# Two transformer blocks in one kernel: the first modulation in column quarters, three projection chunks computed together

## The chip, the cores and the metric

The kernel runs on one core of a Trainium2 chip. Its engines are TensorE (PE in the rows; its loading of weights is PEld), VectorE (DVE), ScalarE (ACT), GpSimd (POOL, unused here) and SyncE (SP), which here does nothing but issue the DMAs. The metric is the device time of one execution, in microseconds (us); less is better.

## The reference

Two blocks run one behind the other on x, 256 rows by 2048. The stretch that changes is the head of the first, with the memory projection of the second, which depends on nothing and is done there too:

```python
# first block
ada = silu(c) @ w_ada + b_ada                    # [2048] @ [2048, 6*2048]
shift_m, scale_m, gate_m, shift_f, scale_f, gate_f = split(ada, 6)
h = rms_norm(x, g_pre_mix) * (1 + scale_m) + shift_m
z = h @ w_in                                     # [256, 2048] @ [2048, 3920]
... mixers (a latent attention and a gated linear attention) on z, w_out, residual, gated FFN
# second block, its memory side
kv = rms_norm(mem_2, ln_mem_2) @ w_xkv_2         # [256, 2048] @ [2048, 1024]
... mixers, cross attention on kv, gated FFN
```

Everything is float32. Each column of `h` needs its own column of shift_m and scale_m, and these need all 2048 rows of `w_ada` (16 k-tiles of 128 rows).

## The kernel before

**Slabs.** All weights come as *slabs* of 1 MB: 128 partitions by 2048 values, four slots (`raw`), one DMA each (`slab`, L398). A slot is issued again once DVE has finished with the slab four places earlier (semaphore `slab_done`). Projection slabs hold four k-tiles of 490 or 512 columns (DMA pieces of about 2 KB); a `w_ada` slab holds one k-tile of 2048 columns (pieces of 8 KB). "A slab" below means one of `w_ada`, "z slab" one of `w_in`, "xkv slab" one of `w_xkv_2`.

**Precision in two halves.** A product in full precision is made of three in a reduced form. ACT rounds a projection slab to `wh` (`hi`, L555), DVE takes the rest, `wl = raw - wh` (`lo`, L1633), and PE adds `wh*XTh`, `wl*XTh` and `wh*XTl` into a bank (`slab_mm`, L1045 to L1047; 24 matmuls a slab, four k-tiles by two row blocks by three). `XTh` and `XTl` are the activations, transposed and split the same way. `wh` and `wl` have two slots each, so ACT rounds a slab only when PE has used the one two before it.

**Modulation.** PE does not multiply `silu(c) @ w_ada`: DVE adds each A slab, scaled by one value of c per partition, to an accumulator of 2048 columns (`ada`, L1650 to L1654), and PE then sums `ACC` over the partitions with 16 one-column products (`mod_sum`, L1082), which DVE turns into shift, gain or gate (`mod_fin`).

**Order around the change.** All of it is written out by hand, for each engine by itself, and every queue runs in order:

1. The rows of mem are normed (ACT, DVE), turned by PE through two banks and split (`turn`, `turn_hi`, `turn_lo`). DVE does eight A slabs before and between.
2. The xkv slabs (two chunks of four), with A slabs of shift_m between those of the first chunk and of scale_m between those of the second. x is normed and turned in this stretch.
3. Seven more A slabs, `mod_sum(1)`, then the gain and shift on the turned x and its split (L1796), all 16 k-tiles.
4. The projection z: eight chunks of 490 columns, four slabs each, a loop of two times four chunks. Two A slabs of gate_m per chunk.
5. Behind it SP issues the slab of `w_uq`, three small loads and `rel_scratch<-relrow`, a 3 MB write of a table to DRAM, and then the 16 A slabs of shift_f. DVE computes rope angles, consumes the first two of these (`ada_some(2)`) and only then copies `aT` out of a bank, on which the gated linear attention's first product (L1146) waits.

## Time and profile before

| | |
|---|---|
| median of 3 runs | 2922.84 us (2920.22 to 2924.76) |
| the profiled execution, its own time | 2926.01 us |
| its span in the profile | 2924.2 us |
| PE busy | 2685.9 us (92%) |
| DVE busy | 1663.4 us (57%) |
| ACT busy | 1157.8 us (40%) |
| mean granted clock of TensorE | 0.954 of full |
| read from HBM | 559.59 MB |

The profile is of one execution. "Idle before" an instruction is the time its engine had nothing to do before it, with what ended that time. The part that changes lies in the first 334 us of the span; what stands behind it is the same code in both kernels, but for semaphore counts.

### The profile page before, as it was taken

The page shows a single profiled execution, that of the slowest core. Times are in us where ns is not written, and L with a number is a line of the kernel's source. Part 1 is how long each engine was busy: PE and PEld are TensorE (multiplying, and loading weights), DVE is VectorE, ACT ScalarE, POOL GpSimd, SP SyncE. Part 2 cuts the span into 40 slices and gives each one's busy share as a digit, 9 for nine tenths or more (in the row PEclk, how much of TensorE's full clock was granted, in tenths as well). Part 3 has the DMA queues.
Part 4 walks back from the last instruction along what each step waited for, and adds up shares of the span by engine and source line. Part 5 has one row for each costly group of instructions (what it writes and reads, how often), then busy time and mean ns, then how long its engine had stood idle before and what let it go on. Part 6 is the DMA issues. An engine that isn't in the chain of part 4 may idle for free.

```text
span 2924.2 us, 31137 instructions
## 1 busy us (share of the span) xinstructions
PE 2685.9 (92%) x12176; PEld 2194.6 (75%) x12176; DVE 1663.4 (57%) x1601; ACT 1157.8 (40%) x1200; POOL 0.2 (0%) x4
## 2 busy tenths in 40 slices
PE   3789769969999999999899999899889999999997
PEld 2578637757888888887788777787667888888886
DVE  6766565855666455555543666555564555555555
ACT  2333244433333333333433444434553333333333
POOL 0000000000000000000000000000000000000000
PEclk9789869979999999999899999999999999999999
DMA  8968843945777555555373444454435555555553
GB/s 329 352 236 286 226 187 110 336 156 189 250 253 260 172 191 192 190 185 171 127 224 118 147 142 132 139 201 160 157 101 185 189 186 187 186 191 192 190 186 129
DMA packets 253356, 565.93 MB, mean 194 GB/s; under 512 B 9647, under 2 KB 52557, under 8 KB 240094
## 3 DMA queue, kind: packets, MB, share of 16 engines
q1 hardware_dynamic: 253278, 564.87, 57.7%
q8 instruction: 52, 0.85, 0.1%
q14 instruction: 26, 0.21, 0.0%
HBM read 559.59 MB, written 5.24 MB: 193 GB/s over the span
## 4 chain that ended last, share of the span: by engine, by line
PE 78%; DVE 8%; ACT 5%; DMA 4%; issue 4%; SPq 1%; DVEq 0%; ACTq 0%
PE bank L1045 23%; PE bank L1047 23%; PE bank L1046 23%; ACT wh L555 3%; DVE wl L1633 2%; DVE ACC L1654 2%; DMA raw<-in_w_ada 2%; DVE ROWB L1633 1%; DMA raw<-in_w_out 1%; DMA raw<-in_w_xkv 1%; PE bank L1016 1%; PE bank L1451 1%; DVE X L1754 1%; PE bank L1503 1%; PE bank L1082 1%
## 5 line engine op out<-in xcount | busy, mean ns | idle before, releaser
L1633 DVE TENSOR_TENSOR wl<-raw,wh 128x2048 fp32r<-128x2048 f32 (+2 forms) x430 | 975.3, 2269 | 912.2 <-ACT wh L555 911.5
L555 ACT ACTIVATE wh<-raw 128x2048 fp32r<-128x2048 f32 (+2 forms) x430 | 816.0, 1898 | 1260.6 <-PE bank L1047 1158.8
L1045 PE MATMUL bank<-wh,XTh 128*128 128x512 f32 (+2 forms) x2712 | 1077.6, 397 | 46.3 <-DVE wl L1633 36.7
L1046 PE MATMUL bank<-wl,XTh 128*128 128x512 f32 (+2 forms) x2712 | 1064.1, 392 | 0.0
L1047 PE MATMUL bank<-wh,XTl 128*128 128x512 f32 (+2 forms) x2712 | 1063.5, 392 | 0.0
L1045 PEld LDWEIGHTS bank<-wh,XTh 128*128 128x128 f32 x2712 | 520.4, 192 | 158.4 <-DVE wl L1633 31.5
L1047 PEld LDWEIGHTS bank<-wh,XTl 128*128 128x128 f32 x2712 | 518.9, 191 | 103.4
L1046 PEld LDWEIGHTS bank<-wl,XTh 128*128 128x128 f32 x2712 | 520.9, 192 | 99.0
L1045 PE MATMUL bank<-wh,HTh 128*128 128x512 f32 x704 | 276.7, 393 | 9.4 <-DVE HTl L1633 3.6
L1047 PE MATMUL bank<-wh,HTl 128*128 128x512 f32 x704 | 274.2, 389 | 0.0
L1046 PE MATMUL bank<-wl,HTh 128*128 128x512 f32 x704 | 274.1, 389 | 0.0
L1045 PEld LDWEIGHTS bank<-wh,HTh 128*128 128x128 f32 x704 | 132.1, 188 | 46.5 <-issue 14.4
L1047 PEld LDWEIGHTS bank<-wh,HTl 128*128 128x128 f32 x704 | 132.2, 188 | 27.7
L1046 PEld LDWEIGHTS bank<-wl,HTh 128*128 128x128 f32 x704 | 132.2, 188 | 26.6
L1654 DVE SCALAR_TENSOR_TENSOR ACC<-raw,cT,ACC 128x2048 f32<-128x2048 f32 x60 | 141.0, 2350 | 7.2 <-DMA raw<-in_w_ada 2.2
L1633 DVE TENSOR_TENSOR ROWB<-ROWB,bank 128x512 f32<-128x512 f32 x176 | 112.6, 681 | 10.9 <-PE bank L1047 9.0
L1650 DVE SCALAR_TENSOR_TENSOR ACC<-raw,cT,ACC 128x2048 f32<-128x2048 f32 x32 | 75.2, 2351 | 4.2 <-DVE wl L1633 1.6
L1016 PE MATMUL bank<-CON,ROWB 128*128 128x128 f32 x96 | 19.1, 355 | 48.2 <-ACT ROWB L548 17.1
L821 ACT ACTIVATE HTh<-bank 128x512 fp32r<-128x512 f32 x44 | 23.9, 595 | 90.4 <-PE bank L1331 90.4
L1016 PEld LDWEIGHTS bank<-CON,ROWB 128*128 128x128 f32 x96 | 14.2, 180 | 53.3 <-ACT ROWB L548 18.0
L548 ACT ACTIVATE XTh<-bank,vT 128x256 fp32r<-128x256 f32 x70 | 28.8, 471 | 47.7 <-PE bank L1016 47.6
L1016 PE MATMUL bank<-CON,X 128*128 128x128 f32 x96 | 19.8, 375 | 27.3 <-DVE X L1754 17.2
(289 smaller groups left out, 1313.4 us busy)
## 6 DMA issues: line engine op xcount, KB each, us to landing
raw<-in_w_ada SPq DMA_DIRECT2D x96, 1024.0 KB, 6.7
raw<-in_w_ffn_gate SPq DMA_DIRECT2D x44, 1024.0 KB, 5.1
raw<-in_w_ffn_up SPq DMA_DIRECT2D x44, 1024.0 KB, 5.2
raw<-in_w_ffn_down SPq DMA_DIRECT2D x44, 1024.0 KB, 5.1
raw<-in_w_gate SPq DMA_DIRECT2D x44, 1024.0 KB, 5.1
raw<-in_w_up SPq DMA_DIRECT2D x44, 1024.0 KB, 5.1
raw<-in_w_down SPq DMA_DIRECT2D x44, 1024.0 KB, 5.1
raw<-in_w_in SPq DMA_DIRECT2D x32, 1024.0 KB, 5.1
```

The costliest lines, as they stand in the source:

```text
L555: act.activation(wh[:, st.lin % 2, 0:width], raw[:, st.raw % 4, 0:width], ACT.Copy).then_inc(hi_made, 1)
L1016: mm = pe.transpose(PB[4 + g % 2][:, SEQ * k + P * r:SEQ * k + P * r + P], src(r, 2 * b + k), ident)
L1045: pe.matmul(out_, hi_t[:, k, rows], w[0][:, q, :], start=first and q == 0, stop=False)
L1046: pe.matmul(out_, hi_t[:, k, rows], w[1][:, q, :], start=False, stop=False)
L1047: mm = pe.matmul(out_, lo_t[:, k, rows], w[0][:, q, :], start=False, stop=last and q == n - 1)
L1082: mm = pe.matmul(PB[7][:, k:k + 1], ACC[:, P * k:P * k + P], ones[:, 0:1], start=True, stop=True)
L1451: pe.matmul(PB[2 + u % 2][:, 0:2 * nk].rearrange("p (b n) -> p b n", b=2), QT(i, par, r), KT2(g, nk), start=True, stop=True).then_inc(S("n ...
L1503: pe.matmul(PB[7][:, HD * b:HD * b + HD], pT[:, u % 2, P * blk_:P * blk_ + P], Z2[:, k, c0:c0 + HD], start=k == 0, stop=k == r)
L1633: return dve.tensor_tensor(out_, a, b, op)
L1650: ins = dve.scalar_tensor_tensor(ACC[:, :], w, cT[:, bass.ds(k0 + k, 1)], ACC[:, :], ALU.mult, ALU.add)
L1654: ins = dve.scalar_tensor_tensor(ACC[:, :], w, cT[:, k:k + 1], ACC[:, :], ALU.mult, ALU.add)
L1754: dve.scalar_tensor_tensor(x, y, nstat[:, j, 2, r:r + 1], x, ALU.mult, ALU.add).then_inc(S("x_added"), 1)
```

## The change

- **A slabs of shift_m and scale_m by column quarters.** A slab is now four k-tiles by 512 columns, in pieces of 2 KB (`ada_part`). DVE handles it in four instructions of 512 columns; even and odd k-tiles go to two partial sums, so that none reads what the one in front of it wrote. Quarter q of the columns is complete after four slabs of each.
- **Sums by quarter.** `mod_parts(q)` sums both, adding the partial sums in the bank: 16 one-column products per quarter. Shift and gain of four k-tiles follow (`mod_part`), then gain and shift on four k-tiles of x by DVE (`h_gained`) and, now computed by ACT for itself from the same numbers, the rounded half (`h_hi`), and `h_lo`.
- **Three chunks together.** Chunks 0 to 2 of z stay open in banks 0 to 5: as soon as a quarter of h is there, its four k-tiles are multiplied with one slab of each of the three chunks. One quarter is: xkv slab, z0, two A, z1, two A, z2, A, xkv slab, three A. The K/V projection of the memory moves to banks 6 and 7. The last five chunks go one after the other, with one A slab of gate_m behind each of the first 16 of their 20 slabs; these loops are written out instead of run as loops.
- **Memory rows turned first.** mem is turned as it is loaded, at once and over four banks, and the norm factor of its rows is applied to the product (`scale=mem_scale(r)`). x is normed behind it and turned over four banks too.

The core of the diff:

```diff
+ZK = 3
+XKV = [(i // 4, i % 4) for i in range(8)]
+WIDE = {"mem", "x"}
+def turn_bank(name, b):
+    return 4 + (b % 4 if name in WIDE else (TURN0[name] + b) % 2)
...
+        def mod_at(q):
+            return PB[5 if q < 3 else 4][:, (496, 496, 504, 496)[q]:(504, 504, 512, 504)[q]]
+        def z_banks(c):
+            return (2 * c, 2 * c + 1) if c <= ZK else (2 * (c % 2), 2 * (c % 2) + 1)
... SP
-            for k in range(8):
-                ada(0, k)
-            for c in range(2):
-                for s in range(4):
-                    cols("w_xkv_2", s, 512 * c, 512)
-                    for k in range(8 + 2 * s, 10 + 2 * s) if c == 0 else range(3 * s, 3 * s + 3):
-                        ada(c, k)
+            def ada_part(v, q, s):
+                slab(W["w_ada"][:, 4 * s:4 * s + 4, v * D + 512 * q:v * D + 512 * q + 512], (4, 512), False)
+            for v in range(2):
+                for s in range(4):
+                    ada_part(v, 0, s)
+                if v == 0:
+                    xkv(0)
+            for q in range(4):
+                xkv(2 * q + 1)
+                for c in range(ZK):
+                    cols("w_in", q, ZC * c, ZC)
+                    if q < 3 and c < 2:
+                        for s in range(2 * c, 2 * c + 2):
+                            ada_part(0, q + 1, s)
+                if q < 3:
+                    ada_part(1, q + 1, 0)
+                    xkv(2 * q + 2)
+                    for s in range(1, 4):
+                        ada_part(1, q + 1, s)
+            for n in range(4 * (ZN - ZK)):
+                cols("w_in", n % 4, ZC * (ZK + n // 4), ZC)
+                if n < KT:
+                    ada(2, n)
... ACT
-            norm_stats("mem", lambda r: MEM[:, r, :], D)
-            norm_rows("mem", lambda r: MEM[:, r, :], lambda r: ROWB[:, r, :])
+            turn_hi("mem", MTh, gain=vT[:, V_LN_MEM:V_LN_MEM + KT])
             act.wait_ge(S("x_in"), 16)
             norm_stats("x", lambda r: X[:, r, :], D)
+            norm_rows("x", lambda r: X[:, r, :], lambda r: XN[:, r, :])
...
+            def h_hi(q):
+                act.wait_ge(S("mod_ready"), 2 * q + 2)
+                for b in (2 * q, 2 * q + 1):
+                    for kt in (2 * b, 2 * b + 1):
+                        ins = act.activation(XTh[:, kt, :], XS[:, kt, :], ACT.Identity, scale=modA[:, 1, kt:kt + 1],
+                                             bias=modA[:, 0, kt:kt + 1])
... PE
+            def mod_parts(q):
+                pe.wait_ge(slab_done, st.raws())
+                for v in range(2):
+                    for k in range(4):
+                        o = mod_at(q)[:, 4 * v + k:4 * v + k + 1]
+                        for par in range(2):
+                            c0 = 512 * (2 * v + par) + P * k
+                            mm = pe.matmul(o, ACC[:, c0:c0 + P], ones[:, 0:1], start=q == 0 and par == 0, stop=par == 1,
+                                           skip_group_check=True)
+                    mm.then_inc(S("mod_sum"), 1)
+            for q in range(4):
+                mod_parts(q)
+                xkv(2 * q + 1)
+                pe.wait_ge(S("x_lo"), 2 * q + 2)
+                for c in range(ZK):
+                    slab_mm(z_banks(c), ALL[4 * q:4 * q + 4], ZC, q == 0, q == 3)
...
+                if q < 3:
+                    st.next(False)
+                    xkv(2 * q + 2)
... DVE
+            def ada_part(v, q, s):
+                dve.wait_ge(landed[st.raw % 4], st.landed())
+                for t in range(4):
+                    part = ACC[:, 512 * (2 * v + t % 2):512 * (2 * v + t % 2) + 512]
+                    w, c = raw[:, st.raw % 4, 512 * t:512 * t + 512], cT[:, 4 * s + t:4 * s + t + 1]
+                    if s == 0 and t < 2:
+                        ins = dve.tensor_scalar(part, w, c, None, ALU.mult)
+                    else:
...
+                        ins = dve.scalar_tensor_tensor(part, w, c, part, ALU.mult, ALU.add)
+            for q in range(4):
+                lo()
+                mod_part(q)
+                h_gained(q)
+                h_lo(q)
+                for c in range(ZK):
+                    lo(4 * ZC)
+                    if q < 3 and c < 2:
+                        for s in range(2 * c, 2 * c + 2):
+                            ada_part(0, q + 1, s)
+                if q < 3:
+                    ada_part(1, q + 1, 0)
+                    lo()
+                    for s in range(1, 4):
+                        ada_part(1, q + 1, s)
```

On DVE, between the last accumulation of scale_m and the first slabs of z, the kernel before has (`XS` the turned x, `modA` shift and gain, `wl` the rest of a weight slab):

```order
L1654 SCALAR_TENSOR_TENSOR ACC<-raw,cT,ACC 128x2048 x7
L1633 TENSOR_TENSOR wl<-raw,wh 128x1960
L1633 TENSOR_TENSOR mtmp<-bank,bT 128x16
L1668 SCALAR_TENSOR_TENSOR modA<-mtmp,vT 128x16
L1796 TENSOR_SCALAR XS<-XS,modA 128x256 x4
L1633 TENSOR_TENSOR XTl<-XS,XTh 128x512
L1796 TENSOR_SCALAR XS<-XS,modA 128x256 x2
```

One quarter's beginning on DVE in the changed kernel (second of the four):

```order
L1719 TENSOR_TENSOR wl<-raw,wh 128x2048 [waits hi_made]
L1719 TENSOR_TENSOR modA<-bank,bT 128x4 [waits mod_sum]
L1719 TENSOR_TENSOR mtmp<-bank,bT 128x4
L1889 SCALAR_TENSOR_TENSOR modA<-mtmp,vT 128x4 [waits dve_step]
L1898 TENSOR_SCALAR XG<-XS,modA 128x256 [waits mod_ready,turn_free]
L1898 TENSOR_SCALAR XG<-XS,modA 128x256 x3
L1719 TENSOR_TENSOR XTl<-XG,XTh 128x512 [waits turn_hi,gained] x2
L1719 TENSOR_TENSOR wl<-raw,wh 128x1960 [waits hi_made]
L1865 TENSOR_SCALAR ACC<-raw,cT 128x512 [waits slab_landed0]
L1865 TENSOR_SCALAR ACC<-raw,cT 128x512
L1873 SCALAR_TENSOR_TENSOR ACC<-raw,cT,ACC 128x512 [waits ada_step] x2
```

The modulation of all 16 k-tiles at once has become four k-tiles at a time, with z slabs and accumulation of the next quarter directly behind.

On SP, the end of the projection before (register instructions of the loop left in):

```order
L398 DMA raw<-in_w_in 128x4x490
L391 REGISTER_ALU
L398 ISA
L398 DMA raw<-in_w_ada 128x2048
L436 REGISTER_ALU
L436 COMPARE_AND_BRANCH
L398 DMA raw<-in_w_uq 128x4x512
```

and in the changed kernel:

```order
L417 DMA raw<-in_w_ada 128x2048
L417 DMA raw<-in_w_in 128x4x490 x4
L417 DMA raw<-in_w_uq 128x4x512
L427 DMA wgu<-in_w_gate_up 16x512
L427 DMA bgr<-in_b_gate 1x512
L427 DMA ggla<-in_g_gla 128x256
L427 DMA rel_scratch<-relrow 2048x1x384
L417 DMA raw<-in_w_ada 128x2048 x16
```

Before, an A slab stood right in front of `w_uq` and another two z slabs before that; now four z slabs stand in front of it with no A slab between.

## Rows read from the trace of the kernel before

**Rows 1.** page of the profile, part 1: busy us, share and instructions

```profile
PE 2685.9 (92%) x12176; PEld 2194.6 (75%) x12176; DVE 1663.4 (57%) x1601; ACT 1157.8 (40%) x1200; POOL 0.2 (0%) x4
```

**Rows 2.** busy us by stretch; then granted clock, DMA share, GB/s

```profile
50.00:100.00 50.00, 36.82 (x147) 29.87 (x148) 38.71 (x22) 19.50 (x17) 0.00 (x0) 0.84 0.79 291
100.00:150.00 50.00, 35.89 (x150) 29.25 (x149) 39.63 (x17) 11.29 (x14) 0.00 (x0) 0.77 1.00 383
200.00:250.00 50.00, 50.00 (x226) 42.05 (x225) 30.14 (x14) 20.26 (x16) 0.00 (x0) 1.00 0.84 292
```

**Rows 3.** timeline, PE, 12 to 165 us: start, length, line, operation, count, idle

```profile
13.52 1.03 PE L1107 MATMUL bank<-onehot,rbT 32*16 32x256 f32 x2 [0.32 <-DVE rbT L1764]
31.64 1.97 PE L1016 MATMUL bank<-CON,ROWB 128*128 128x128 f32 x8 [17.09 <-ACT ROWB L548]
54.37 0.77 PE L1045 MATMUL bank<-wh,XTh 128*128 128x512 f32 x1 [5.15 <-DVE wl L1633]
58.77 0.63 PE L1046 MATMUL bank<-wl,XTh 128*128 128x512 f32 x1
59.20 0.63 PE L1047 MATMUL bank<-wh,XTl 128*128 128x512 f32 x1
...
143.05 6.99 PE L1082 MATMUL bank<-CON,ACC 128*128 128x1 f32 x32 [3.31 <-DVE ACC L1654]
154.11 0.77 PE L1045 MATMUL bank<-wh,XTh 128*128 128x490 f32 x1 [4.07 <-DVE XTl L1633]
```

**Rows 4.** timeline, DVE, 15 to 330 us

```profile
125.92 17.08 DVE L1654 SCALAR_TENSOR_TENSOR ACC<-raw,cT,ACC 128x2048 f32<-128x2048 f32 x7
...
152.54 0.73 DVE L1796 TENSOR_SCALAR XS<-XS,modA 128x256 f32<-128x256 f32 x2
153.18 0.68 DVE L1633 TENSOR_TENSOR XTl<-XS,XTh 128x512 fp32r<-128x512 f32 x1
...
196.14 2.20 DVE L1633 TENSOR_TENSOR wl<-raw,wh 128x1960 fp32r<-128x1960 f32 x1 [2.98 <-ACT wh L555]
...
217.64 2.20 DVE L1633 TENSOR_TENSOR wl<-raw,wh 128x1960 fp32r<-128x1960 f32 x1 [2.98 <-ACT wh L555]
```

**Rows 5.** timeline, PE, around the end of the input projection

```profile
333.75 4.51 PE L1082 MATMUL bank<-CON,ACC 128*128 128x1 f32 x32
...
364.82 2.04 PE L1146 MATMUL bank<-wgu,aT 16*128 16x512 f32 x2 [16.92 <-DVE aT L1841]
```

**Rows 6.** timeline, the DMA-issuing queue on SP, same place

```profile
320.08 0.38 SPq L398 DMA_DIRECT2D raw<-in_w_uq  x1
...
321.77 0.69 SPq L408 DMA_DIRECT2D rel_scratch<-relrow  x1
```

**Rows 7.** DMA issues, 318 to 362 us: count, size, us to landing

```profile
rel_scratch<-relrow SPq DMA_DIRECT2D x1, 3072.0 KB, 35.0
```

**Rows 8.** timeline, DVE, 322 to 450 us

```profile
325.14 2.20 DVE L1633 TENSOR_TENSOR wl<-raw,wh 128x1960 fp32r<-128x1960 f32 x1 [2.98 <-ACT wh L555]
...
359.62 1.29 DVE L1652 TENSOR_SCALAR ACC<-raw,cT 128x2048 f32<-128x2048 f32 x1 [18.24 <-DMA raw<-in_w_ada]
...
364.27 0.41 DVE L1841 COPY aT<-bank 16x256 f32<-16x256 f32 x1
...
377.87 0.43 DVE L1847 TENSOR_SCALAR la<-la 128x512 f32<-128x512 f32 x1
...
388.51 0.68 DVE L1856 SCALAR_TENSOR_TENSOR Z<-Z,eb 128x512 f32<-128x512 f32 x1
389.11 0.68 DVE L1633 TENSOR_TENSOR kd<-Z,kd 128x512 f32<-128x512 f32 x1
```

**Rows 9.** timeline, ACT, one slab's rounding

```profile
83.05 1.91 ACT L555 ACTIVATE wh<-raw 128x2048 fp32r<-128x2048 f32 x1 [7.19 <-DMA raw<-in_w_xkv]
```

**Rows 10.** DMA queues, 100 to 142 us: packets, MB, share of 16 engines

```profile
q1 hardware_dynamic: 3416, 15.97, 98.7%
```

**Rows 11.** DMA queues, 2500 to 2800 us (slabs in 2 KB pieces only)

```profile
q1 hardware_dynamic: 28576, 56.73, 58.3%
```

More of the change, by code:

```diff
@@ L658, in _ @@
                 act.wait_ge(S("turned"), g + 1)
[L659 to L667 removed]
+                f(XS[:, 2 * b:2 * b + 2, :].rearrange("p t n -> p (t n)"), PB[turn_bank("x", b)][:, :], ACT.Copy, "turn_free")
@@ L675, in _ @@
+            for n in range(4 * (ZN - ZK)):
+                hi(4 * ZC)
+                if n < ZK:
+                    z_evac(n, 18 + n)
+                if n % 4 == 1 and n > 4:
+                    z_evac(ZK + n // 4 - 1, st.lin - 2)
+                skip(n < KT)
+            hi()
+            z_evac(ZN - 1, st.lin - 1)
             for b in range(4):
@@ L1813, in _ @@
+            for n in range(4 * (ZN - ZK)):
+                lo(4 * ZC)
+                if n < KT:
+                    ada(n)
+            lo()
             dve.wait_ge(S("pos_in"), 16)
```

263 lines of the change are left out of this document (140 added, 123 removed).

## The prediction

> **What bounds the kernel now.** I read the page first: PE is busy 2685.9 us of the span of 2924.2 [rows 1], so over the whole kernel PE is the bound, and a change at its head can only win what PE loses there. Next the busy time by stretch: between 50 and 150 us PE is busy 36.8 and 35.9 of each 50 us, at a granted clock of 0.84 and 0.77, while the DMA engines are at 0.79 and 1.00; between 200 and 250 us PE is busy 50.00 of 50 at 1.00 and DMA stands at 0.84 [rows 2]. So there are two regimes: up to about 150 us the weights of the modulation come in and PE has too little to do; then the projection z runs at PE's pace with DMA to spare. The timeline of PE gives the border: one-column sums at 143.05 (6.99 us long), first z matmul at 154.11 after 4.07 us idle [rows 3]; that of DVE shows seven A slabs back to back from 125.92 in 17.08 us [rows 4], with nothing for PE beside them. One period of the z loop is 217.64 - 196.14 = 21.50 us for four slabs [rows 4], 5.375 us a slab; 32 of them are 172.0 us, and the stretch from 154.11 to the next sums at 333.75 [rows 5] is 179.6. I call this last time E, the end of the projection. Behind it PE waits again: L1146 starts at 364.82 after 16.92 us idle [rows 5]. It waits for aT (DVE, 364.27), which stands behind two A slabs, of which the first found DVE idle for 18.24 us until 359.62 [rows 8]; and that slab was queued behind the 3 MB write, issued at 321.77 [rows 6] and 35.0 us from issue to landing [rows 7].
>
> **Until the last A slab of scale_m is done (T).** 20 z slabs are left for the regime of PE, 12 go into the regime of DMA and DVE. The question is how much longer the second gets.
>
> Start: PE is free to turn mem once L1107 (13.52, 1.03 us) is through, at 14.6 instead of 31.64 [rows 3]. Turning two blocks costs 1.97 us of PE [rows 3], eight blocks 7.9; four banks let PE run through, and DVE's last piece follows about 2 us later: 24.6. Behind it DVE has eight A slabs, x's second row block (an estimate from four times as many columns as the 0.43 of a 512-wide scaling [rows 8], about 1.4), one lo (2.29) and a wait for ACT, which has two squares of 2048 columns to do, each like its 1.91 [rows 9]: about 1.5.
>
> Price of an A slab on DVE: in the old form 17.08 / 7 = 2.44 us [rows 4]. In the new form four instructions of 512 columns. Two such that don't read each other start 389.11 - 388.51 = 0.60 apart, though each lasts 0.68 [rows 8]; four are 2.42, the same as before. Where a quarter opens, two are plain scalings of 0.43 [rows 8], a slab is then about 1.9. So eight slabs are 2 x 1.9 + 6 x 2.42 = 18.3 us, and the first two groups end at 24.6 + 18.3 + 1.4 + 2.3 + 1.5 = 48.1 us.
>
> Here the Trainium skill speaks against the change: "VectorE: DVE Perf Modes", section "The TRN2 errata — SBUF-src ops pay a fixed extra latency per instruction", puts about 151 cycles on top of N in an fp32 instruction, once per instruction, so many small ones pay it many times. By that a slab of four would be 4 x 0.69 = 2.76 us where one of 2048 columns is 2.3. The durations in this trace agree with it (0.68 for 512 columns), the distance between starts (0.60) doesn't; it becomes a rival below.
>
> One quarter, counted from its last A slab. PE sums 16 columns: 4.51 to 6.99 us for x32 rows of the same count [rows 5, 3]; near the lower end with the hand-over, 4.2. DVE does the lo of the xkv slab meanwhile. Then shift and gain 0.65, four scalings (0.73 for two, [rows 4]) and two subtractions (0.68 each) 3.2 with their hand-overs, 0.5 waiting for ACT's rounding, lo of z0 2.3: 10.8 us after the quarter's start DVE gives back z0's slot. For some 5 us of this nothing new can be issued, all four slots being full or waiting. From there DMA rules: 2.1 us until data flow (an estimate), then eight slabs until the quarter's last A slab, and that slab's 2.45 on DVE. DVE alone would need 36.5 us for the quarter (eight A slabs 18.4, five lo 11.6, the modulation's 6.5 without the lo counted already).
>
> Price of a slab on DMA: between 100 and 142 us, saturated, 15.97 MB at 98.7% of the span, 385 GB/s, 2.72 us for 1.05 MB; most of these are pieces of 8 KB [rows 10]. Late in the kernel, with 2 KB pieces only, 56.73 MB took 58.3% of 300 us, 324 GB/s or 3.23 us, but there the queue is never full and a packet's time holds waits [rows 11]. A slabs now come in 2 KB too. I take 2.9, nearer to the saturated row, and keep 2.7 and 3.2 as ends. A quarter is then 10.8 + 2.1 + 8 x 2.9 + 2.45 = 38.5 us; with 1 us more for sums that PE makes at the slow clock, 39.5.
>
> PE's own work in a quarter is the sums (4.5), two xkv slabs and three z slabs of 5.4: 31.5 at full clock. The first slab after the idle 5.15 us starts at 54.37 with 0.43 us from matmul to matmul (58.77 to 59.20), against 0.224 in the z loop [rows 3, 4]: the lower of the clock's two levels, 1.2 GHz, for the first 12 of its 24. With one such start per slab PE would need 5 x 7.9 + 7 = 46.5 us, more than the 39.5; but a PE that is behind has no idle time in front of its slabs, and so keeps the clock. I leave it out of the sum and in the range.
>
> T = 48.1 + 3 x 39.5 = 166.6, say 168 with PE late at the first sums.
>
> **From T to E.** Sums 4.5, xkv slab 5.4, 3 + 20 z slabs 23 x 5.375 = 123.6, and 3.5 for a start at the lower clock and the wait for the last quarter's h: E = 168 + 137 = 305. Before it was 333.75. Gain 28.8 us. In this tail 20 z slabs of 1.0 MB and 16 A slabs must come in 107 us: 36.9 MB, 343 GB/s, 89% of the saturated row; DVE needs 4.7 of each 5.375 and ACT 1.9 [rows 9]. Both stay just under PE.
>
> **Behind E.** The slot of `w_uq` was given back by an A slab with two z slabs still to come (320.08 [rows 6], E - 13.7). Now it is given back by the lo of the fourth z slab from the end. The last lo ended at 325.14 + 2.20 = 327.34 [rows 8], E - 6.4; three slabs earlier is E - 22.5. So the 3 MB write starts 8.8 us earlier against E, in a stretch where no other slab is waiting, and the A slab behind it lands as much earlier. PE's other condition, the sums and the bank with aT's source, is met by about E + 14, while aT came at E + 30.5; the idle 16.92 us cover the whole 8.8. I count 9. What follows is the same chain, shifted.
>
> Removed at no gain of its own: the reset of ACC and the loops' register work; they lay in the stretches counted. mem's norm factor moves from rows to the product's evacuation, no more work for ACT.
>
> **Sum.** Profiled execution 2926.01 - 28.8 - 9 = 2888.2. The median of the runs stands 3.2 us under that execution: 2885.
>
> **The rivals.**
> 1. *DMA hides, DVE alone sets the quarters.* If slabs take 2.7 us and are there when wanted, T = 48.1 + 3 x 36.5 = 158 and E 295: 2875. For it: the 8 KB rows at 385 GB/s. Against it: the 5 us per quarter in which all slots are held. 0.12.
> 2. *Every slab starts at the lower clock*, as at 54.37. The quarters are then PE's, 46.5 us, 21 us more: 2906. For it: clock 0.77 and 0.84 where slabs come one by one [rows 2]. Against it: being late ends the idle time. 0.15. The skill has the mechanism too ("TensorE: Matmul & The Clock Gate", section "HAM oscillation — how this bites in real kernels"): bursts with waits for data between them start cold each time.
> 3. *DVE's pieces cost their full duration*, 4 x 0.68 [rows 8] = 2.72 us an A slab, 0.30 more in the slabs on the path, some 24 of them: 7 us, 2892. 0.07. (It is the rule weighed above; its own 0.69 would give 8 us.)
> 4. *Slower*: PE stays at the lower clock all through the quarters. A slab is then 24 x 0.43 = 10.3 us, a quarter 5 x 10.3 + 7 = 58.5, three of them 57 us more: 2885 + 57 = 2942. It decides from a quarter of 52.2 us, a slab of 9.0 us. Against it: in the stretches of rows 2 with the same spacing of slabs the clock was 0.77 to 0.84 and not 0.5. 0.06.
> 5. *No effect outside what can be told* (a comparison of this kernel tells some 0.2%, 6 us): several of the costs add up, as 3.2 us a slab on DMA in quarters and tail, the write no earlier, and half of rival 2. 0.05.
>
> My forecast, DMA and slots setting the quarters, has 0.55 (2872 to 2899): with 2.7 us a slab it is 2880, with 3.2 us 2892 and some 5 us more in the tail, which then wants more than DMA gives. The range of 8 in 10 takes in rival 1 and rival 2: 2868 to 2908. Faster by over 0.2%: 0.55 + 0.12 + 0.15 + 0.07 = 0.89; within 0.05; slower 0.06.
>
> **What would show it.** In the changed profile: mem turned from about 15 us; the first z matmul at about 60 instead of 154; the one-column sums in four places about 39 us apart, from about 48; after the last of them PE without a gap until E at about 305; DMA share near 0.95 in between. The spacing of DVE's 512-wide accumulations shows 0.60 or 0.68. `rel_scratch` issued at E - 21, and aT at about E + 21. I am wrong if the sums are 46 us apart or more (look then at the clock in these stretches), if PE shows gaps in the last five chunks (DMA), or if L1146's successor still starts 31 us after E.

## The result, and the profile after

| | before | after |
|---|---|---|
| median of 4 runs | 2923.11 us (2920.22 to 2924.76) | 2893.65 us (2891.42 to 2898.32) |
| ratio, 95% interval | | 0.9902 (0.989 to 0.9915) |
| the profiled execution | 2926.01 us | 2898.32 us |
| its span | 2924.2 us | 2896.5 us |

The kernel became 29.5 us faster where 38 were forecast; 2893.65 lies in the range (2868 to 2908), 8.65 us above the forecast. In the profiled executions the gain is 27.7 us, and nearly all of it stands by L1232, the L1146 of before: it starts at 339.51 instead of 364.82, 25.3 us earlier.

Part 1 of the page after, which answers to [rows 1]: PE is still the bound, with 5.7 us more busy time. The four rows of one-column sums take 20.7 us of PE where the two of before took 10.8; behind E the added work ends, and PE has 4.2 us less.

```profile
PE 2691.6 (93%) x12240; PEld 2201.6 (76%) x12240; DVE 1667.4 (58%) x1704; ACT 1158.0 (40%) x1207; POOL 0.2 (0%) x4
```

Busy time by stretch, after, the answer to [rows 2]. In the first two PE has 8.8 and 5.7 us more to do than before; in the third it was busy 50.00 of 50 and is 49.53 now, while DMA went from 0.84 to 0.95:

```profile
50.00:100.00 50.00, 45.61 (x190) 37.90 (x190) 39.98 (x58) 15.12 (x14) 0.00 (x0) 0.84 0.87 312
100.00:150.00 50.00, 41.58 (x185) 34.10 (x185) 39.01 (x55) 15.30 (x14) 0.00 (x0) 0.90 0.83 295
200.00:250.00 50.00, 49.53 (x222) 41.44 (x221) 39.59 (x18) 19.68 (x17) 0.00 (x0) 1.00 0.95 341
```

The timeline of PE, after, the answer to [rows 3, 5]. The first row is mem's turning (31.64 before), the next four the sums of the four quarters, then E and the wait behind it:

```profile
14.05 6.17 PE L1069 MATMUL bank<-CON,MEM 128*128 128x128 f32 x32
...
46.50 6.99 PE L1172 MATMUL bank<-CON,ACC 128*128 128x1 f32 x32 [3.53 <-DVE ACC L1873]
...
89.54 3.73 PE L1172 MATMUL bank<-CON,ACC 128*128 128x1 f32 x32 [0.79 <-DVE ACC L1873]
...
134.57 3.96 PE L1172 MATMUL bank<-CON,ACC 128*128 128x1 f32 x32
...
174.37 6.01 PE L1172 MATMUL bank<-CON,ACC 128*128 128x1 f32 x32 [1.06 <-DVE ACC L1873]
...
315.33 3.63 PE L1134 MATMUL bank<-CON,ACC 128*128 128x1 f32 x32
...
339.51 2.04 PE L1232 MATMUL bank<-wgu,aT 16*128 16x512 f32 x2 [9.55 <-DVE aT L1968]
```

So the quarters took 43.0, 45.0 and 39.8 us, T is 174.4 and T to E 141.0. The timeline of DVE, after, the answer to [rows 4, 8]:

```profile
106.67 5.39 DVE L1873 SCALAR_TENSOR_TENSOR ACC<-raw,cT,ACC 128x512 f32<-128x512 f32 x8
113.02 2.20 DVE L1719 TENSOR_TENSOR wl<-raw,wh 128x1960 fp32r<-128x1960 f32 x1 [0.96 <-ACT wh L586]
...
124.28 2.29 DVE L1719 TENSOR_TENSOR wl<-raw,wh 128x2048 fp32r<-128x2048 f32 x1 [6.94 <-ACT wh L586]
126.49 8.03 DVE L1873 SCALAR_TENSOR_TENSOR ACC<-raw,cT,ACC 128x512 f32<-128x512 f32 x12
...
201.21 2.20 DVE L1719 TENSOR_TENSOR wl<-raw,wh 128x1960 fp32r<-128x1960 f32 x1 [3.15 <-ACT wh L586]
...
291.53 2.20 DVE L1719 TENSOR_TENSOR wl<-raw,wh 128x1960 fp32r<-128x1960 f32 x1 [1.50 <-ACT wh L586]
...
334.28 1.29 DVE L1738 TENSOR_SCALAR ACC<-raw,cT 128x2048 f32<-128x2048 f32 x1 [11.29 <-DMA raw<-in_w_ada]
...
338.96 0.41 DVE L1968 COPY aT<-bank 16x256 f32<-16x256 f32 x1
```

Three things are to be read here. Eight 512-wide accumulations take 5.39 us, 0.67 each, though none reads what the one in front of it wrote: an A slab costs 2.7 us and not 2.42. (E is the start of the sums behind the last z slab, as before; T is read at the start of the fourth quarter's sums, right behind the last A slab of scale_m.) In the middle quarter DVE stands idle for 6.94 us in front of the second xkv slab, with three A slabs behind it that make the quarter's end. And between 201.21 and 291.53 there are 16 pairs of a z slab and an A slab, 5.645 us each, where one z slab takes PE 5.375 [rows 4].

The write, after, by the queue of SP and by the list of DMA issues (290 to 345 us), against [rows 6, 7]: issued at E - 19.9, where it was E - 12.0, and as long as before.

```profile
295.44 0.69 SPq L427 DMA_DIRECT2D rel_scratch<-relrow  x1
```

```profile
rel_scratch<-relrow SPq DMA_DIRECT2D x1, 3072.0 KB, 35.2
```

### The profile page after: what moved, and what is told of

It reads as the page before. It is cut to its first block, busy times and chain, and to the rows that moved or that the text cites. A ratio compares the mean times of both kernels' runs of the same rounds, so it can differ in the third digit from the quotient of the medians.

```text
span 2896.5 us, 31089 instructions
## 1 busy us (share of the span) xinstructions
PE 2691.6 (93%) x12240; PEld 2201.6 (76%) x12240; DVE 1667.4 (58%) x1704; ACT 1158.0 (40%) x1207; POOL 0.2 (0%) x4
## 4 chain that ended last, share of the span: by engine, by line
PE 75%; DVE 10%; DMA 5%; ACT 5%; issue 4%; SPq 1%; DVEq 0%; ACTq 0%
PE bank L1098 22%; PE bank L1100 22%; PE bank L1099 22%; ACT wh L586 4%; DVE wl L1719 3%; DMA raw<-in_w_in 2%; DVE ACC L1873 2%; DVE ROWB L1719 1%; DMA raw<-in_w_out 1%; DMA raw<-in_w_ada 1%; PE bank L1069 1%; PE bank L1537 1%; DMA raw<-in_w_xkv 1%; DVE X L1842 1%; PE bank L1589 1%
## 5 line engine op out<-in xcount | busy, mean ns | idle before, releaser
L1098 PE MATMUL bank<-wh,XTh 128*128 128x512 f32 (+2 forms) x2648 | 1046.2, 395 | 33.2 <-DVE wl L1719 28.4
L1100 PE MATMUL bank<-wh,XTl 128*128 128x512 f32 (+2 forms) x2648 | 1034.4, 391 | 0.0
L1099 PE MATMUL bank<-wl,XTh 128*128 128x512 f32 (+2 forms) x2648 | 1034.0, 390 | 0.0
L1098 PEld LDWEIGHTS bank<-wh,XTh 128*128 128x128 f32 x2648 | 505.0, 191 | 141.1 <-DVE wl L1719 28.3
L1100 PEld LDWEIGHTS bank<-wh,XTl 128*128 128x128 f32 x2648 | 503.7, 190 | 99.8
L1099 PEld LDWEIGHTS bank<-wl,XTh 128*128 128x128 f32 x2648 | 505.4, 191 | 95.8
L1098 PEld LDWEIGHTS bank<-wh,HTh 128*128 128x128 f32 x704 | 132.1, 188 | 46.4 <-issue 14.4
L1740 DVE SCALAR_TENSOR_TENSOR ACC<-raw,cT,ACC 128x2048 f32<-128x2048 f32 x45 | 105.7, 2349 | 4.7 <-DMA raw<-in_w_ada 1.1
L1873 DVE SCALAR_TENSOR_TENSOR ACC<-raw,cT,ACC 128x512 f32<-128x512 f32 x112 | 75.5, 746 | 0.0
L1069 PEld LDWEIGHTS bank<-CON,X 128*128 128x128 f32 x96 | 15.8, 193 | 31.5 <-issue 18.3
L1736 DVE SCALAR_TENSOR_TENSOR ACC<-raw,cT,ACC 128x2048 f32<-128x2048 f32 x16 | 37.6, 2350 | 1.8 <-DVE wl L1719 0.9
L579 ACT ACTIVATE JUNK<-ROWB 128x512 f32<-128x512 f32 x40 | 24.9, 628 | 31.1 <-DVE ROWB L1719 31.1
```

Source lines behind the costliest of these rows:

```text
L1069: mm = pe.transpose(PB[turn_bank(name, b)][:, SEQ * k + P * r:SEQ * k + P * r + P], src(r, 2 * b + k), ident)
L1098: pe.matmul(out_, hi_t[:, k, rows], w[0][:, q, :], start=first and q == 0, stop=False)
L1099: pe.matmul(out_, hi_t[:, k, rows], w[1][:, q, :], start=False, stop=False)
L1100: mm = pe.matmul(out_, lo_t[:, k, rows], w[0][:, q, :], start=False, stop=last and q == n - 1)
L1736: ins = dve.scalar_tensor_tensor(ACC[:, :], w, cT[:, bass.ds(k0 + k, 1)], ACC[:, :], ALU.mult, ALU.add)
L1740: ins = dve.scalar_tensor_tensor(ACC[:, :], w, cT[:, k:k + 1], ACC[:, :], ALU.mult, ALU.add)
```

## The experiments

All but e9 start from the changed kernel, and their times are held against its 2893.65 us, or by their ratios to the kernel before, which ran beside each of them. One caution for single profiles: e7 and e8 have the changed kernel's instructions up to T, and their T is 177.27 and 174.32 against its 174.37, with middle quarters of 48.8, 44.9 and 45.0. A difference in T below 3 us says nothing, and neither does one below 4 us in the middle quarter. The medians were taken beside kernels before of 2921.59 to 2925.43 us, so a difference of two of them carries a few us of that too.

### What sets the length of a quarter: e1 to e4

**e1: ACT rounds first.** In the middle quarter the idle 6.94 us come through ACT's queue. Its timeline, after: the rounding of the second xkv slab stands behind two evacuations of `xkT`, and these wait for PE to turn the keys, which PE does behind z2.

```profile
111.14 1.84 ACT L586 ACTIVATE wh<-raw 128x1960 fp32r<-128x1960 f32 x1 [7.13 <-DMA raw<-in_w_in]
121.36 1.09 ACT L579 ACTIVATE xkT<-bank 128x512 f32<-128x512 f32 x2 [8.38 <-PE bank L1204]
122.34 1.91 ACT L586 ACTIVATE wh<-raw 128x2048 fp32r<-128x2048 f32 x1
```

```diff
... ACT, in the loop over q
-                if q == 1:
-                    for b in range(2):
-                        act.wait_ge(S("xk_turned"), b + 1)
-                        f(xkT[...], PB[6 + b][:, :], ACT.Copy, "xk_out")
                 if q < 3:
                     skip()
                     hi()
                     skip(3)
+                if q == 1:
+                    (the same four lines)
```

> The changed kernel, but in the second quarter ACT rounds the xkv slab behind the three z slabs before it evacuates the turned K (two copies that wait for PE), not after. Theory (a wait in ACT's queue): DVE's idle 6.94 us before that slab's subtraction falls to the 1.2 to 1.4 us of the other quarters, the last A slab of scale_m ends at 174.4 - 5.6 = 168.8, the projection ends at about 309.7, and the kernel is 5 to 6 us faster than the changed one: 2888. Rival (the slab or DMA was late anyway): the idle time turns up before the next slabs and 0 to 2 us are won.

Measured: 2893.45 us (2887.73 to 2901.57), ratio 0.989 (0.9864 to 0.9917). The wait did go, 6.94 became 1.10 (timeline of DVE, e1):

```profile
121.92 2.29 DVE L1719 TENSOR_TENSOR wl<-raw,wh 128x2048 fp32r<-128x2048 f32 x1 [1.10 <-ACT wh L586]
```

but the middle quarter is 44.9 us as before, since z2 came later (timeline of PE, e1; PE waited 4.21 us for it, 2.85 without the edit):

```profile
118.76 0.78 PE L1098 MATMUL bank<-wh,XTh 128*128 128x490 f32 x1 [4.21 <-DVE wl L1719]
```

The two parts of the quarter must be told apart. From its sums to z2 nothing differs between e1, e7, e8 and the changed kernel, for the edit stands behind z2 in ACT's queue; yet this part took 29.4 us in e1, 27.9 in e7, and 25.6 and 25.7 in e8 and the changed kernel. The granted clock in it was 0.81 and 0.82 in the two long ones, 0.93 in the two short ones. Behind z2, where the edit acts, the changed kernel and e8 take 19.3 us, e7 20.9 and e1 15.5. So the wait was on the chain and some 4 us went with it; a slower start that the edit didn't make hid them. In the median it is nothing that can be told: 0.2 us, where 5 to 6 were expected.

**e2: two banks** for turning mem and x, as before the change.

```diff
-WIDE = {"mem", "x"}
+WIDE = set()
```

> The changed kernel, with mem and x turned over two banks instead of four. Theory: turning mem takes 8 x 1.48 us (period of the kernel before: 2.95 for two blocks) instead of 6.2 on PE, DVE starts its first A slab 5 us later (22.6 to 27.7), and the end moves by about as much: 4 to 5 us slower than the changed kernel. Rival: DMA, which is the slower partner from there on, has its four slots full at 22 us either way and makes it good: under 1 us.

Measured: 2900.13 us (2897.47 to 2903.35), ratio 0.992 (0.9903 to 0.9936). The first sums start at 50.61 instead of 46.50 and T is 3.4 us later, but E is 315.16, the same. In the profiled execution the tail took back what the head lost (T to E 137.4 instead of 141.0); the median is 6.5 us worse, but the intervals overlap. Four banks are worth 4 us at the first sums; whether they arrive at the end stays open.

**e3: half the bytes** of every A slab of the last three quarters (two of its four k-tiles aren't loaded).

```diff
-                slab(W["w_ada"][:, 4 * s:4 * s + 4, ...], (4, 512), False)
+                n = 2 if q else 4
+                slab(W["w_ada"][:, 4 * s:4 * s + n, ...], (n, 512), False)
```

> The changed kernel, but the 24 A slabs of quarters 1 to 3 load only two of their four k-tiles (half the bytes; DVE works on what stands in the slot, so shift and gain are not the reference's). Theory (DMA and slots set the quarters): the quarters shrink from 43.1, 44.9 and 39.9 us to what DVE needs, 37 to 38 (41 with the wait of the turned K). Rival (DVE's pieces set them): they shrink by 1 us or less each.

**e4: half the work of DVE** on the same slabs (two of four accumulations left out).

```diff
-                for t in range(4):
+                last = 1 if q else 3
+                for t in range(last + 1):
```

> The changed kernel, but DVE accumulates only two of the four k-tiles of the 24 A slabs of quarters 1 to 3 (DMA unchanged; leaves half of that sum out). Theory (DMA sets the quarters): they become what DMA needs, 13 slabs x 2.85 = 37 us, plus the part in which all slots are held: 39 to 40. Rival (DVE): DVE's work falls by 8 x 1.3 = 10.6 us a quarter, to 29 to 32 us.

Measured: one run each, 2900.95 and 2897.23 us; T 177.17 and 175.72, against 174.37. The busy time between 55 and 175 us of the changed kernel, e3 and e4, in this order (third column group DVE, at the end clock, DMA share, GB/s):

```profile
55.00:175.00 120.00, 102.04 (x435) 82.97 (x434) 99.22 (x133) 35.07 (x30) 0.00 (x0) 0.90 0.88 316
```

```profile
55.00:175.00 120.00, 103.96 (x420) 85.04 (x420) 97.19 (x130) 33.17 (x29) 0.00 (x0) 0.84 0.66 211
```

```profile
55.00:175.00 120.00, 102.11 (x426) 84.43 (x425) 68.08 (x83) 33.47 (x29) 0.00 (x0) 0.86 0.86 312
```

DMA falls to 0.66 and 211 GB/s, or DVE to 68 us of 120, and the three quarters together last 130.7 (e3) and 129.5 us (e4), against 127.9. Singly they are 43.8, 47.4 and 39.5, and 40.8, 49.4 and 39.3; only the first of e4 is shorter than in any run with the same order of slabs, by 1 us or more. Quarters of 37 to 38 and of 29 to 32 us were to be seen if one rate alone set them, so neither does alone. PE's busy time is 102 to 104 us of 120 in all three. What these runs leave open is several limits of nearly equal length: with one eased, the others still hold the quarter. No run eased two at once.

### Taking a link out of the chain: e5, e6, e11

After e1 to e4 my theory was that a quarter is a chain, each link of which waits for the one before: sums, shift and gain, h, z0, z1, the slot that z2 needs, its way from issue to landing, z2, the second xkv slab, the last A slabs.

**e5: two chunks together instead of three.** (The last quarter's sums are added to what a bank already holds, so four k-tiles of h aren't the reference's; number and kind of the instructions are as intended.)

```diff
-ZK = 3
+ZK = 2
```

> Two chunks are computed together instead of three: each quarter has one z slab less, the tail 24 z slabs instead of 20. Theory (a quarter is a chain that runs through PE's slabs, their slots and their landing, one z slab is one link of it): the quarters shrink from 42.6 to about 38.5 us, T (end of the last A slab of scale_m) comes some 12 us earlier, and T to E has three chunks' last quarter less one slab (-5.4) and four tail slabs more (+21.5), with A slabs in 16 of 24 tail slabs, so that the last pairs are not held up by DMA (-3): E about +1 to +2 us against the changed kernel, 2895. Rival (DMA's or DVE's throughput sets the quarters): one slab less of nine saves 2.9 us a quarter on DMA, 2.2 on DVE, T 9 or 7 us earlier, E +4 to +7, 2900.

Measured: 2895.37 us (2887.97 to 2900.61), ratio 0.9907 (0.9891 to 0.9924). The sums of e5:

```profile
46.57 6.99 PE L1172 MATMUL bank<-CON,ACC 128*128 128x1 f32 x32 [3.60 <-DVE ACC L1873]
...
86.86 4.04 PE L1172 MATMUL bank<-CON,ACC 128*128 128x1 f32 x32
...
123.93 3.73 PE L1172 MATMUL bank<-CON,ACC 128*128 128x1 f32 x32
...
160.97 3.63 PE L1172 MATMUL bank<-CON,ACC 128*128 128x1 f32 x32
...
312.56 4.22 PE L1134 MATMUL bank<-CON,ACC 128*128 128x1 f32 x32
```

The quarters are 40.3, 37.1 and 37.0, T is 13.4 us earlier where 12 were expected. But that sum doesn't bear the theory out. The first and the third quarter are each 2.8 us shorter, which is a slab's time on DMA (2.9) and half of its time on PE (5.4); the middle one is 8.0 us shorter, because the long wait of e1 went there too (DVE's idle in front of the second xkv slab is 1.90 us instead of 6.94). T to E grows by 10.6 us, and E comes 2.8 us earlier where 1 to 2 later was expected; the median shows nothing of it. How many chunks run together decides little here: what leaves a quarter comes back in the tail.

**e6: another order in the quarter**, with ACT's order of e1.

```diff
+NA = (1, 1, 3)
... SP; the same on ACT, PE and DVE
-                    if q < 3 and c < 2:
-                        for s in range(2 * c, 2 * c + 2):
-                            ada_part(0, q + 1, s)
+                    if q < 3:
+                        for _ in range(NA[c]):
+                            v, s = next(parts)
+                            ada_part(v, q + 1, s)
                 if q < 3:
-                    ada_part(1, q + 1, 0)
                     xkv(2 * q + 2)
-                    for s in range(1, 4):
-                        ada_part(1, q + 1, s)
+                    for v, s in parts:
+                        ada_part(v, q + 1, s)
```

> Same work, ACT's rounding of the quarter's first slab first (as e1), and the order of a quarter is xkv, z0, A, z1, A, z2, three A, xkv, three A instead of xkv, z0, two A, z1, two A, z2, A, xkv, three A. z2 then takes the slot that z0's lo gives back, not that of the second A slab: it can be issued about 5 us earlier. Theory (chain by slots and landing): PE's gaps of 3 to 4.5 us before z2 go, quarters of about 39.5 instead of 42.6, T and E 6 to 9 us earlier, 2886. Rival (the clock or something else sets the quarters, or another link takes over at once, as in e1): quarters stay over 42, E within 3 us of 313 to 315, 2892.

Measured: 2892.59 us (2891.72 to 2894.76), ratio 0.9891 (0.9875 to 0.9906). Quarters of 43.7, 40.8 and 41.4, T 172.27, E 310.86:

```profile
130.92 3.96 PE L1173 MATMUL bank<-CON,ACC 128*128 128x1 f32 x32 [0.51 <-DVE ACC L1873]
...
310.86 3.63 PE L1135 MATMUL bank<-CON,ACC 128*128 128x1 f32 x32
```

PE's gap in front of z2 is gone (four slabs run without a break, 94.06 to 118.55), and the middle quarter loses 4.2 us; e10, which has the same order, has 40.9 there, and no run with the old order has less than 44.9 (e5 with its missing slab aside). It needn't be the new order, though: behind z2 e1 won as much by ACT's order alone, and no run has the new order without it. In the other quarters the new order won nothing. The first is 43.7 (42.7 in e10, 43.0 in the changed kernel), and the last grew to 41.4 (42.5 in e10, against 39.8): PE's gap is gone in front of z2 and is back in front of the second xkv slab, 6.40 us long. Of the 6 to 9 us expected 4.5 came at E and 1 in the median, which is the rival's 2892.

**e11: more work for PE in front of its gaps.** z1 and z2 of the first three quarters also get the product `wl*XTl`.

```diff
... slab_mm, with fourth=q < 3 and c > 0 where z0 to z2 are multiplied
+                        if fourth:
+                            pe.matmul(out_, lo_t[:, k, rows], w[1][:, q, :], start=False, stop=False)
```

> The changed kernel, in which the slabs z1 and z2 of the first three quarters also get the fourth product wl*XTl (8 matmuls of 490 columns more a slab, 1.8 us at full clock, 16 a quarter). They lie in front of PE's gaps of 3 to 5 us (before z2 and before the second xkv slab). Theory (in a quarter PE falls to 1.2 GHz for 6 to 10 of 24 matmuls behind each such gap, some 3 us of the 42.6): the gaps shrink to 1 to 3 us, at least one of the two slow stretches goes, a quarter stays as long or gets 1 to 2 us shorter in spite of 3.6 us more PE work, T 0 to 5 us earlier, 2889 to 2894. Rival (the clock is not on the chain, but PE's work is): each quarter up to 3.6 us longer, T 5 to 11 us later, 2899 to 2904. Third (neither: gaps simply absorb the work, slow stretches stay): T within 2 us, 2893.

Measured: 2898.72 us (2893.63 to 2902.95), ratio 0.9918 (0.9904 to 0.9932); quarters 42.6, 49.5 and 40.0, T 178.53, E 315.17. The first and third took in 16 more matmuls (3.6 us at full clock) without getting longer, so PE's time on z1 and z2 isn't on the chain there. In the first PE was busy only 0.8 us more, because 6 of its matmuls ran at the lower clock instead of 22; in the third 3.4 us more, with 13 instead of 14. The middle one is 4.5 us longer than that of the changed kernel, but e7 has 48.8 there without the products. Its idle in front of the second xkv slab stayed 4.95 us, and 9 matmuls behind z2 ran at the lower clock, as ten did in the changed kernel.

What the lower clock costs can be read from e7 against the changed kernel, which have the same instructions up to T. Busy time in the middle quarter of the changed kernel and of e7 (the third value from the end is the granted clock), and the sums that end this quarter in e7:

```profile
90.00:135.00 45.00, 36.33 (x162) 29.56 (x161) 34.69 (x47) 14.59 (x14) 0.00 (x0) 0.89 0.86 307
```

```profile
90.00:135.00 45.00, 37.05 (x143) 30.79 (x143) 31.46 (x42) 11.57 (x13) 0.00 (x0) 0.77 0.78 277
...
137.96 3.67 PE L1172 MATMUL bank<-CON,ACC 128*128 128x1 f32 x32
```

Of the 119 recorded slab matmuls of that quarter 17 ran at the lower clock in the changed kernel (0.63 us each instead of 0.39), 18 in e8 and 33 in e7, and the quarter took 45.0, 44.9 and 48.8 us. The 16 more account for 3.4 us of the 3.8 (an estimate, at 0.21 us each), so there the clock is on the chain. In the first quarter 22 and 15 went with 43.0 and 42.7 us, in the third 14 and 8 with 39.8 and 39.3: there it is nearly all absorbed.

### The tail: e7

```diff
             for n in range(4 * (ZN - ZK)):
                 cols("w_in", n % 4, ZC * (ZK + n // 4), ZC)
-                if n < KT:
-                    ada(2, n)
+                if n % 5 < 4:
+                    ada(2, n - n // 5)
```

> The 16 A slabs of gate_m are spread over all 20 z slabs of the last five chunks (none behind every fifth) instead of one behind each of the first 16. Theory (in the tail DMA sets the pace of 5.645 us per pair where PE needs 5.375): all 20 slabs at 5.375 or a little over, E 3 to 4.5 us earlier than 315.3. But w_uq's slot now comes back later against E (behind three z slabs and an A slab instead of four z slabs), rel_scratch is issued about E-14 instead of E-19.9, so of it 3 to 6 us are lost again behind E: the end within 3 us of the changed kernel, 2890 to 2896. Rival (the tail's extra time is PE's start at the lower clock and not DMA): E unchanged, the end 3 to 6 us later, 2899.

Measured: 2900.57 us (2897.77 to 2904.56), ratio 0.9921 (0.9908 to 0.9934). The tail did what the theory says. Busy time of e7 in its tail, PE 105.97 of 106 us at DMA 0.93, against 87.69 of 90 at 0.97 in the changed kernel:

```profile
203.00:309.00 106.00, 105.97 (x476) 89.58 (x476) 80.09 (x36) 42.22 (x33) 0.00 (x0) 1.00 0.93 329
```

```profile
201.00:291.00 90.00, 87.69 (x391) 73.06 (x390) 71.77 (x32) 34.81 (x29) 0.00 (x0) 1.00 0.97 350
```

T to E is 135.7 us, 5.3 less, E 312.95 though T was 2.9 us later. (This shows that a z slab and an A slab side by side cost more than PE's pace; whether by DMA's rate or by the slots isn't told apart.) And behind E it lost more: the write was issued at 300.06, E - 12.9, and DVE waited 17.62 us for the first A slab of shift_f (timeline of DVE, e7):

```profile
338.24 1.28 DVE L1738 TENSOR_SCALAR ACC<-raw,cT 128x2048 f32<-128x2048 f32 x1 [17.62 <-DMA raw<-in_w_ada]
```

aT stands at E + 30.0 where the changed kernel has E + 23.6. So 6.3 us are lost for 2.4 won at E; the median is worse than expected (2890 to 2896), at the figure that the rival gave for another reason. A gain in front of a transfer that is placed by its queue can be worth less than nothing.

### Behind E: e8 and e9

**e8: the write elsewhere.**

```diff
... SP, behind the slab of w_uq and the three small loads
-            sp.wait_ge(S("rel_row"), 2)
-            load("rel_out", rel_d, relrow[:, :].unsqueeze(1).broadcast_to([NH, P, REL_W]))
... in the loop that issues w_out and scale_f
+                    if (c, s) == (0, 1):
+                        sp.wait_ge(S("rel_row"), 2)
+                        load("rel_out", rel_d, relrow[:, :].unsqueeze(1).broadcast_to([NH, P, REL_W]))
```

> The 3 MB write of rel_scratch is issued later, behind the second A slab of scale_f among the w_out slabs, where DMA has idle time, instead of in front of the 16 A slabs of shift_f. Theory (behind E PE waits for aT, aT for two A slabs, these for the write in front of them in the queue): E unchanged, first A slab of shift_f done by E+10 instead of E+19, aT at about 330 instead of 339, the whole end 9 us earlier: 2884.5. Rival 1 (PE is held there by something else as well, a_turned's source or the sums): 2 to 4 us. Rival 2 (the write now delays slabs where it stands): the gain at L1232 is 9 us, but given back by the last add, 2893 or slower.

**e9: the same move alone, in the kernel before.**

> The kernel before, with only the write of rel_scratch moved behind the second A slab of scale_f, as in e8. Theory: the gain of the change behind E (6.9 us) is nothing but the write's earlier issue against E; with the write out of the way it is gone, and before gains more than the changed kernel did: aT comes 14 us after E in both, 364.3 to about 348, the end 16 us earlier, 2907. Difference to e8 then is E's alone, about 19 to 22 us (2907 against 2885). Rival (something of the change itself shortens the stretch behind E): before gains no more than e8 did, 9 us: 2914.

Measured: e8 2884.87 us (2876.84 to 2892.33), ratio 0.9865 (0.9846 to 0.9884); e9 2905.09 us (2902.18 to 2905.58), ratio 0.9939 (0.9927 to 0.9951). The timeline of DVE, e8: both A slabs have landed when DVE is free, and aT now waits for its source on PE, the other condition:

```profile
321.73 1.29 DVE L1739 TENSOR_SCALAR ACC<-raw,cT 128x2048 f32<-128x2048 f32 x1
323.13 2.35 DVE L1741 SCALAR_TENSOR_TENSOR ACC<-raw,cT,ACC 128x2048 f32<-128x2048 f32 x1
327.82 0.41 DVE L1969 COPY aT<-bank 16x256 f32<-16x256 f32 x1 [2.34 <-PE bank L1228]
```

The gate's first product on PE, e8 and then e9:

```profile
328.38 1.09 PE L1233 MATMUL bank<-wgu,aT 16*128 16x512 f32 x2 [0.59 <-DVE aT L1969]
```

```profile
348.57 1.09 PE L1147 MATMUL bank<-wgu,aT 16*128 16x512 f32 x2 [0.59 <-DVE aT L1842]
```

It starts at E + 14.4 and E + 14.7, so the stretch behind E is the same in both kernels once the write is gone, and what is left between them is E: 20.2 us at this product, and 20.2 us in the medians. The kernel before gains 16.5 us (against its neighbour's 2921.59) by one moved transfer, over half of what the whole change brought, and the changed one 8.8 by the medians (10.8 by the two ratios, and 13.4 between the two profiled executions; e8's runs spread over 15 us). Both came within 2 us of the expectation.

### All three: e10

e6, e7 and e8 in one kernel.

> e6, e7 and e8 together: quarter in the order xkv, z0, A, z1, A, z2, three A, xkv, three A; gate_m's A slabs spread over all 20 tail slabs; rel_scratch written behind the second A slab of scale_f. Theory: E 4 us (order) and 3 to 5 us (tail) earlier than 315.3, about 307 to 309; what e7 lost behind E was the write, which is no longer there, so nothing is lost: aT at E+14 = 322, 17 us earlier than in the changed kernel: 2877. Rival (the two shortenings of the tail and quarters are one and the same slack): E 311, 2881.

Measured: 2876.16 us (2872.82 to 2878.38), ratio 0.9843 (0.983 to 0.9857), 17.5 us under the changed kernel: the fastest version, and the expectation (2877) was met. E and the gate's product of e10:

```profile
306.34 3.63 PE L1136 MATMUL bank<-CON,ACC 128*128 128x1 f32 x32
...
320.24 1.09 PE L1233 MATMUL bank<-wgu,aT 16*128 16x512 f32 x2 [0.60 <-DVE aT L1970]
```

T to E is 133.7 us, PE busy 100.00 of 100. Against e6 the even tail takes 4.9 us off it (138.6), and E and the gate's product are both 8 us earlier than in e8: what cost time in e7 is a gain once the write no longer stands behind it. Between 200 and 300 us, busy time of e10:

```profile
200.00:300.00 100.00, 100.00 (x451) 84.83 (x450) 77.09 (x34) 40.33 (x31) 0.00 (x0) 1.00 0.96 349
```

## Why the prediction was right, and where its terms were off

In the large the mechanism was as forecast: 20 z slabs near PE's pace behind T, E earlier, the write earlier against E, then the same chain shifted. What the forecast said of the quarters, that DMA's rate sets them from the held slots on, isn't what the runs show, and by a sign of its own ("if PE shows gaps in the last five chunks") it was wrong of the tail. Term by term:

| | forecast | measured | off by |
|---|---|---|---|
| first sums | 48.1 | 46.50 | -1.6 |
| PE late at the first sums | 1.4 | none | -1.4 |
| three quarters | 3 x 39.5 = 118.5 | 127.87 (42.6 each) | +9.4 |
| T | 168 | 174.37 | +6.4 |
| T to E | 137 | 140.96 | +4.0 |
| E (gain) | 305 (28.8) | 315.33 (18.4) | +10.3 |
| gain behind E, at aT | 8.8 | 6.9 | +1.9 |

Together 12 us at aT; by the last instruction the profiled execution is 10.1 us above its own forecast (2898.32 against 2888.2), since about 2 us came back later, and the median is 8.65 above 2885. That it is no more is in part luck: the first sums came 3.0 us earlier than counted, 2 us came back in a stretch that the forecast left alone, and the median stands 4.7 us under the profiled execution where 3.2 were counted.

**The quarters** are the mis-sized term: 39.5 us each were counted, 43.0, 45.0 and 39.8 came. "From there DMA rules: 2.1 us until data flow, then eight slabs" put them down to DMA's rate, and rival 1 to that of DVE. e3 and e4 show that neither counts alone. No row shows the 2.1 us either; what the trace has is the whole way of a slab. z2 of the middle quarter takes the slot that the second A slab gives back, is issued at 104.68, and ends ACT's wait for it at 111.14, 6.5 us later:

```profile
104.68 0.37 SPq L417 DMA_DIRECT2D raw<-in_w_in  x1
```

I had counted the 5 us of held slots once, at the quarter's opening; here they occur a second time. PE's gap in front of z2 in the middle quarter is 2.85 us, in front of the second xkv slab 4.95:

```profile
115.27 0.49 PE L1098 MATMUL bank<-wh,XTh 128*128 128x490 f32 x1 [2.85 <-DVE wl L1719]
...
126.72 0.77 PE L1098 MATMUL bank<-wh,MTh 128*128 128x512 f32 x1 [4.95 <-DVE wl L1719]
```

As the cause of the missing 3.1 us a quarter this is argued and not shown: e6 took the gap in front of z2 away, and the first and the third quarter got no shorter by it. Nor does PE's price of a slab explain them (e5 gave back 2.8 us a quarter and not 5.4; e11 added 3.6 and cost nothing in two quarters). In the middle quarter two parts can be read, ACT's order (some 4 us behind z2, e1) and the clock. What holds the first and the third stays open; that DMA and DVE each need nearly the whole of them (in the third the DMA share is 0.92, and DVE is busy 34 of 39.8 us) fits e3, e4, e5 and e11, and would be tested by easing both at once.

Rival 2 was half true. Its price was 46.5 us if every slab started at the lower clock, 1.2 GHz; in the changed kernel 22, 17 and 14 matmuls of the three quarters ran so, of 119 recorded in each (the granted clock is 0.90 in the second row of the stretches). "A PE that is behind has no idle time in front of its slabs, and so keeps the clock" didn't hold behind the sums: with 0.25 us of idle in front of it the first xkv slab started at the lower clock.

```profile
93.52 0.79 PE L1098 MATMUL bank<-wh,MTh 128*128 128x512 f32 x1 [0.25 <-DVE wl L1719]
```

For this the sum had 1 us a quarter, for sums at the slow clock, and nothing for the slabs. In the middle quarter that was too little: 16 more such matmuls in e7 went with 3.8 us more. In the other two the clock shows no price.

**The pieces of DVE.** "Two such that don't read each other start 0.60 apart" [rows 8] was a pair of different operations. In a row of accumulations they start 0.67 apart, and each lasts 0.75 (112 of them in the changed kernel's trace). Rival 3 had the figure (0.68), though not for its reason, the full duration; and the trace of before held the row; I took a row that was near in size, not in form. This is the last row of that timeline (DVE, the kernel before):

```profile
2915.48 5.39 DVE L1754 SCALAR_TENSOR_TENSOR X<-ROWB,nstat,X 128x512 f32<-128x512 f32 x8
```

It cost nothing that can be seen, though: with half the pieces (e4) the quarters are no shorter. The Trainium skill ("VectorE: DVE Perf Modes", section "The TRN2 errata — SBUF-src ops pay a fixed extra latency per instruction"), by whose rule a piece takes 0.69 and a slab 2.76 us (an estimate from the rule), was close to the 2.70 that the trace shows, though the accumulations last 0.75 and not 0.69. The mistake was to hold the pair at 0.60 against it.

**The tail** was off by the price of a slab that I had used myself. At 2.9 us a slab a pair needs 5.8 us, more than PE's 5.375; I compared 343 GB/s with the saturated 385 instead [rows 10] and called it 89%. It is 5.645 a pair, DMA at 0.97, 16 x 0.27 = 4.3 us: the +4.0 of T to E. e7 shows it by taking it away; that DMA's rate is the reason, and not the slots that wait in front of each transfer, is argued from its share alone.

**The write** was issued 7.9 us earlier against E, not 8.8, and then stood beside the last z slabs; 6.9 arrived. e9 and e8 confirm the reading of the whole place: aT can come at E + 14, as the prediction had it ("met by about E + 14"), and what the change gained behind E was a part of the 16 us that lay there.

Rival 4 (PE at 1.2 GHz all through) didn't occur: the granted clock was 0.84 and 0.90 of full in the stretches, not 0.5. Rival 5 is out by the interval.

## What to carry to other kernels

- When two engines and the DMA all stand at 80 to 90% in a stretch, don't take one rate for the limit: write down one period as a chain, with every slot's giver and every transfer's way from issue to landing. Halving each suspect's work in a run of its own tells whether it counts alone; it takes a run that halves two at once to tell whether they hold the stretch together.
- Hold periods against each other one by one and part by part, not by their mean. The mean of e5 (4.5 us) looked like PE's price, and was 2.8, 8.0 and 2.8; e1 looked like no gain, and had one in the part where the edit acts.
- Use one price throughout. A slab's price that makes the quarter DMA's must be laid against PE's pace in the tail as well.
- Look at what a large transfer in an in-order queue stands in front of before rebuilding the code around it: moving one write gave the kernel before 16.5 us, and decided whether e7's 5 us were worth having.

## What the hardware showed that I hadn't expected

- VectorE's pace depends on the form of what stands in a row: 512-wide instructions of 0.68 us start 0.60 apart where two of different operations stand together [rows 8], those of 0.75 us 0.67 apart in rows of eight accumulations (5.39 us).
- The idle time in front of the gate's product had a second price: behind 9.55 us of idle its two matmuls take 2.04 us, behind 0.59 us they take 1.09 (e8, e9; rows above). The granted clock was 0.50 in the first case and 1.00 in e8: PE had fallen to the lower level in the wait. e9 is 16.3 us earlier than before at aT and 20.2 at the next `mod_sum` (443.29 to 423.12); how much of the difference is the clock's isn't told apart.
- The write of `rel_scratch` holds its queue far longer than its bytes say. DMA busy share in tenths and GB/s from 290 to 345 us, 40 slices, after:

```profile
DMA  9999999988888888888888888888999999999899
GB/s 326 351 335 403 387 356 306 206 123 102 96 96 98 95 101 94 108 99 96 98 95 101 94 98 97 96 104 118 263 400 417 435 417 435 411 435 405 334 393 405
```

  The DMA engines are 0.8 busy at some 98 GB/s, against 400 behind it, and the A slab behind it ends DVE's wait only at 334.28.
- Code that is the same up to T gave 44.9, 45.0 and 48.8 us for the middle quarter in three profiles, with 18, 17 and 33 matmuls at the lower clock. A chain of waits with the clock in it has a spread of its own; a single profile settles 3 us of it neither way.
- Rows of one-column products don't keep TensorE's clock up: behind 3.7 to 7.0 us of them, with at most 0.25 us of idle between, the next slab starts with matmuls of 0.63 us instead of 0.39 (at 53.35, 93.52 and 138.40 in the changed kernel).
